# A Hymba-style block: queries and values projected 512 columns wide in K halves, in a new chunk order, with the F, Q and G weights split once and kept in DRAM

## What is computed

```python
h = rmsnorm(x, norm1_w)
proj = h @ w_in                                 # 1024 x 2816
qa, ka, va, qb, fb, ib, gb = split(proj)        # 512, 128, 128, then four of 512
ya = swa_sink_attention(qa, ka, va, ...)        # 8 query heads, 2 key/value heads of 64, window of two 64-token chunks
yb = hgrn2(qb, fb, ib, gb, ...)                 # 4 heads of 128: gated linear recurrence, chunkwise
x = x + concat(ya, yb) @ w_out
gate, up = split(rmsnorm(x, norm2_w) @ w_gate_up)
x = x + (silu(gate) * up) @ w_down              # inner width 2816
```

## Time and profile before

| | us |
|---|---|
| median of 3 runs (lowest, highest) | 2134.61 (2134.19, 2135.76) |
| the profiled execution | 2135.83 |
| its span, first to last instruction | 2134.0 |
| PE busy in the span | 2099.1 |
| DVE busy | 1377.9 |
| ACT busy | 886.0 |
| block 1, from qT 0 at 235.72 to that of block 2 at 402.21 | 166.5 |

### The profile page before, as it was taken

How to read it: one execution, slowest core, us unless ns; L and a number is a source line. 1 busy time by engine, 2 the same in 40 slices (tenths; PEclk the granted TensorE clock), 3 DMA queues, 4 the chain that set the end, 5 groups by cost and what they waited for, 6 DMA issues and landing times.

```text
span 2134.0 us, 28560 instructions
## 1 busy us (share of the span) xinstructions
PE 2099.1 (98%) x11128; PEld 1771.7 (83%) x11128; DVE 1377.9 (65%) x2034; ACT 886.0 (42%) x1490; POOL 105.5 (5%) x108
## 2 busy tenths in 40 slices
PE   7999999999999998999999999999999999999999
PEld 7889879879978787888888888888888888888887
DVE  6666667666577885777777677777677754444332
ACT  5684685585585333432332334333333332222221
POOL 3100200201100000000000000000000000000000
PEclk9999999999999999999999999999999999999999
DMA  7323422523326675444445344645445575654532
GB/s 280 130 75 124 165 80 85 199 80 104 134 86 216 204 263 203 163 133 145 152 158 173 96 146 168 217 143 178 151 144 178 170 253 185 205 179 167 181 134 90
DMA packets 176662, 338.10 MB, mean 158 GB/s; under 512 B 10448, under 2 KB 105936, under 8 KB 161552
## 3 DMA queue, kind: packets, MB, share of 16 engines
q1 hardware_dynamic: 170016, 305.60, 42.4%
q0 software_dynamic: 6512, 30.67, 4.0%
HBM read 233.99 MB, written 102.24 MB: 158 GB/s over the span
## 4 chain that ended last, share of the span: by engine, by line
PE 60%; DVE 0%; DVEq 0%; ACT 0%; issue 0%
PE b_bank_A L351 4%; PE b_bank_A L350 4%; PE b_bank_A L352 4%; PE b_bank_C L351 4%; PE b_bank_B L351 4%; PE b_bank_C L352 4%; PE b_bank_B L350 4%; PE b_bank_C L350 4%; PE b_bank_B L352 4%; PE b_hx_bank L1932 3%; PE b_hx_bank L1930 3%; PE b_hx_bank L1931 3%; PE b_bank_D L350 2%; PE b_bank_D L351 2%; PE b_bank_D L352 2%; PE b_hx_bank L1875 1%
## 5 line engine op out<-in xcount | busy, mean ns | idle before, releaser
L1816 ACT ACTIVATE b_s_hi<-b_s_stage 128x1408 fp32r<-128x1408 f32 x56 | 77.4, 1383 | 300.2 <-PE b_hx_bank L1932 143.7
L350 PE MATMUL a_pj<-a_w_hi,a_hT_hi 128*128 128x256 f32 x640 | 185.7, 290 | 1.5 <-DVE a_hT_lo L1202 1.5
L351 PE MATMUL a_pj<-a_w_lo,a_hT_hi 128*128 128x256 f32 x640 | 181.0, 283 | 0.0
L352 PE MATMUL a_pj<-a_w_hi,a_hT_lo 128*128 128x256 f32 x640 | 180.9, 283 | 0.0
L350 PE MATMUL a_pj<-a_hT_hi,a_w_hi 128*128 128x512 f32 x384 | 154.6, 403 | 6.4 <-ACT a_gT L871 6.0
L352 PE MATMUL a_pj<-a_hT_hi,a_w_lo 128*128 128x512 f32 x384 | 150.1, 391 | 0.0
L351 PE MATMUL a_pj<-a_hT_lo,a_w_hi 128*128 128x512 f32 x384 | 150.0, 391 | 0.0
L350 PE MATMUL b_bank_A<-b_h_hi_B,b_w_hi 128*128 128x512 f32 x352 | 137.9, 392 | 0.0
L351 PE MATMUL b_bank_A<-b_h_lo_B,b_w_hi 128*128 128x512 f32 x352 | 137.5, 391 | 0.0
L350 PE MATMUL b_bank_B<-b_h_hi_T,b_w_hi 128*128 128x512 f32 x352 | 137.3, 390 | 0.0
L352 PE MATMUL b_bank_A<-b_h_hi_B,b_w_lo 128*128 128x512 f32 x352 | 137.3, 390 | 0.0
(11 more groups left out here) (309 smaller groups left out, 5151.6 us busy)
## 6 DMA issues: line engine op xcount, KB each, us to landing
b_gu_stage<-w_gu SPq DMA_DIRECT2D x44, 1024.0 KB, 5.2
a_w_stage<-w_whole SPq DMA_DIRECT2D x40, 1024.0 KB, 5.0
b_s_stage<-a_sums SPq DMA_DIRECT2D x56, 704.0 KB, 4.1
a_sums<-b_a SPq DMA_DIRECT2D x88, 256.0 KB, 5.4
a_sums<-b_gate SPq DMA_DIRECT2D x66, 256.0 KB, 3.9
b_hx<-hc POOLq DMA_DIRECT2D x12, 1024.0 KB, 5.5
b_w_blocks<-w_dn SPq DMA_DIRECT2D x11, 1024.0 KB, 4.9
o_x<-x_pad SPq DMA_DIRECT2D x16, 512.0 KB, 5.3
```

The source lines that it names most:

```text
L350: pe.matmul(out, stationary[0](k), moving[0](k), start=(k == 0 and not adds), stop=False, skip_group_check=adds)
L351: pe.matmul(out, stationary[0](k), moving[1](k), start=False, stop=False, skip_group_check=adds)
L352: last = pe.matmul(out, stationary[1](k), moving[0](k), start=False, stop=(k == ends), skip_group_check=adds)
L1816: act.activation(f.s_hi[n % 2][:], f.s_stage[n % 2][:], ACT.Copy).then_inc(f.s_hi_ready, 1)
```

## The change

**Chunks.** QA0 and QA1 become QAl and QAh: all 512 query columns, first for the lower half of K (4 k), then the upper; I01 and I23 become Il and Ih in the same way. A group has 12 matmuls of 512 columns with the same 128 tokens standing still, and the four groups of a pair stay open in four PSUM banks until the second half is added: `a_pj0`, `a_pj1`, `a_sc0`, `a_sc1` for the queries, `a_pv`, `a_hb`, `a_pj0`, `a_pj1` for the values. pv 0 and att 0, which use `a_pv` and `a_hb`, therefore wait for the eviction of Ih's groups 0 and 1. ACT evicts 512 columns at once, four times instead of eight. The query columns are permuted on the host.

**Kept weights.** In block 0 the chunks F0, F1, F23, Q01, Q23, G01 and G23 are loaded and split as before, and SP then stores w_hi and w_lo to DRAM. In blocks 1 to 3 SP loads both parts from there straight into w_hi and w_lo (kept_load), once PE has finished chunk n - 2; the step stands where the split would. KV, QAl, QAh, Il and Ih are loaded and split in every block.

**Order.** All splits and kept loads now stand at their automatic place; none is placed by hand. o 2 moves to the next block's first group, and the steps are spread over the new chunks as shown. `junk`, the discard tile of the squares, gets a place of its own.

```diff
-CHUNKS = [("KV", 512, 256), ("QA0", 0, 256), ("QA1", 256, 256), ("F0", 1280, 128), ("F1", 1408, 128),
-          ("Q01", 768, 256), ("I01", 1792, 256), ("G01", 2304, 256), ("F23", 1536, 256), ("Q23", 1024, 256),
-          ("I23", 2048, 256), ("G23", 2560, 256)]
+CHUNKS = [("KV", 512, 256), ("QAl", 0, 512), ("QAh", 0, 512), ("F0", 1280, 128), ("F1", 1408, 128), ("F23", 1536, 256),
+          ("Q01", 768, 256), ("Il", 1792, 512), ("Ih", 1792, 512), ("Q23", 1024, 256), ("G01", 2304, 256), ("G23", 2560, 256)]
...
-    after("I01", 0, ("ha", 0), ("split_hi", CHUNK_AT["G01"]))
-    after("I01", 1, ("sm2", 0), ("sm2", 1), ("sc", 1), ("split_lo", CHUNK_AT["G01"]))
-    after("I01", 2, ("pt", 0), ("pt", 1), ("sm1", 2), ("sm1", 3), ("hb", 0))
-    after("I01", 3, ("sm2", 2), ("sm2", 3), ("pv", 0), ("sc", 2))
...
-    after("G01", 3, ("ds", 0, 0), ("ds", 0, 1), ("sm2", 6), ("sm2", 7), ("pv", 2), ("hc", 1))
-    after("F23", 1, ("o", 0), ("on1", 0), ("kt", 1), ("pt", 6), ("pt", 7), ("ha", 2), ("sq", 0))
-    after("Q23", 0, ("pv", 3), ("on2", 0), ("hb", 2), ("split_lo", CHUNK_AT["I23"]), ("ds", 1, 0), ("ds", 1, 1), ("att", 1), ("sq", 1))
-    after("Q23", 1, ("yt", 0), ("hc", 2), ("sq", 2))
-    after("I23", 0, ("o", 1), ("on1", 1), ("ha", 3), ("sq", 3))
-    after("I23", 1, ("on2", 1), ("n1a",), ("kt", 2), ("hb", 3), ("split_lo", CHUNK_AT["G23"]))
-    after("I23", 2, ("yt", 1), ("att", 2), ("hc", 3))
-    after("I23", 3, ("n1b", 0), ("n1b", 1), ("n1b", 2), ("n1b", 3))
-    after("G23", 0, ("ds", 2, 0), ("ds", 2, 1), ("split_hi", NW), ("split_lo", NW))
-    after("G23", 1, ("xT", 0), ("xT", 1))
...
+    after("F23", 0, ("qT", 0), ("qT", 1), ("kT",))
+    after("F23", 1, ("qT", 2), ("qT", 3))
+    after("Q01", 0, ("sc", 0), ("xload",))
+    after("Q01", 1, ("sm1", 0), ("sm1", 1))
+    after("Il", 0, ("ha", 0))
+    after("Il", 1, ("sm2", 0), ("sm2", 1), ("sc", 1), ("hb", 0))
+    after("Il", 2, ("pt", 0), ("pt", 1), ("sm1", 2), ("sm1", 3))
+    after("Il", 3, ("hc", 0), ("ha", 1))
+    after("Ih", 0, ("sm2", 2), ("sm2", 3), ("sc", 2), ("hb", 1))
+    after("Ih", 1, ("pv", 0), ("kt", 0))
+    after("Ih", 2, ("pt", 2), ("pt", 3), ("att", 0), ("sm1", 4), ("sm1", 5))
+    after("Ih", 3, ("hc", 1), ("sm2", 4), ("sm2", 5), ("sq", 0))
+    after("Q23", 0, ("pv", 1), ("ds", 0, 0), ("ds", 0, 1), ("sc", 3), ("sq", 1))
+    after("Q23", 1, ("pt", 4), ("pt", 5), ("o", 0), ("on1", 0), ("sm1", 6), ("sm1", 7), ("ha", 2))
+    after("G01", 0, ("sm2", 6), ("sm2", 7), ("pv", 2), ("on2", 0), ("kt", 1), ("hb", 2))
+    after("G01", 1, ("pt", 6), ("pt", 7), ("att", 1), ("sq", 2), ("hc", 2))
+    after("G01", 2, ("yt", 0), ("ds", 1, 0), ("ds", 1, 1), ("pv", 3), ("ha", 3), ("hb", 3))
+    after("G01", 3, ("kt", 2), ("sq", 3), ("n1a",), ("hc", 3))
+    after("G23", 0, ("o", 1), ("on1", 1), ("n1b", 0), ("n1b", 1), ("n1b", 2), ("n1b", 3))
+    after("G23", 1, ("on2", 1), ("xT", 0), ("xT", 1))
+    after("G23", 2, ("att", 2), ("yt", 1), ("ds", 2, 0), ("ds", 2, 1), ("xT", 2), ("xT", 3))
+    after("G23", 3, ("kt", 3), ("xT", 4), ("xT", 5), ("xT", 6), ("xT", 7))
...
+        following = (b, n + 1) if n + 1 < NW else (b + 1, 0)
+        first_steps = [("split_hi", n + 1), ("split_lo", n + 1)] if following in RAW else [("kept_load", n + 1)] if n + 1 < NW else []
...
+        def store_kept(n):
+            for tile, to in kept_parts(n):
+                sp.dma_start(to, tile).then_inc(w_kept[n % 2], 16)
+
+        def load_kept(b, n):
+            sp.wait_ge(pj_full.sem, pj_full.upto(b, GROUPS_TO[n - 1]))
...
+            for tile, of in kept_parts(n):
+                sp.dma_start(tile, of).then_inc(w_kept[n % 2], 16)
...
+                    elif name in K_HALF:
+                        first_k = K_HALF[name] * (KT // 2)
+                        wide_hi, wide_lo = (part[s][:].rearrange("p a c -> p (a c)") for part in (w_hi, w_lo))
+                        last = three_passes(pe, bank[:], still,
+                                            (lambda k: wide_hi[:, (k - first_k) * 512:(k - first_k + 1) * 512],
+                                             lambda k: wide_lo[:, (k - first_k) * 512:(k - first_k + 1) * 512]), range(first_k, first_k + KT // 2))
```

More of the change, by code:

```diff
@@ L58, with raw_count, staged_count, next_staged @@
 WHOLE_CHUNKS = [n for n in range(NW) if n not in HALF_CHUNKS]
+K_HALF = {"QAl": 0, "Il": 0, "QAh": 1, "Ih": 1}
+SPLIT_ONCE = [n for n, c in enumerate(CHUNKS) if c[0] in FIRST_HEAD]
+RAW = [(b, n) for b in range(NB) for n in range(NW) if b == 0 or n not in SPLIT_ONCE]
+STAGED = [[chunk for chunk in RAW if chunk[1] % 2 == s] for s in range(2)]
+def raw_count(b, n):
+    return RAW.index((b, n)) + 1
+def staged_count(b, n):
+    return STAGED[n % 2].index((b, n)) + 1
+def next_staged(b, n):
+    same = STAGED[n % 2]
+    at = same.index((b, n)) + 1
+    return same[at] if at < len(same) else None
+def kept_count(b, n):
+    s = n % 2
+    return sum(32 for bb in range(b + 1) for m in SPLIT_ONCE if m % 2 == s and (bb < b or m <= n))
 def chunk_name(n):
@@ L113, in block_steps @@
-    after("I23", 2, ("yt", 1), ("att", 2), ("hc", 3))
-    after("I23", 3, ("n1b", 0), ("n1b", 1), ("n1b", 2), ("n1b", 3))
-    after("G23", 0, ("ds", 2, 0), ("ds", 2, 1), ("split_hi", NW), ("split_lo", NW))
-    after("G23", 1, ("xT", 0), ("xT", 1))
-    after("G23", 2, ("o", 2), ("on1", 2), ("kt", 3), ("xT", 2), ("xT", 3))
-    after("G23", 3, ("xT", 4), ("xT", 5), ("xT", 6), ("xT", 7))
-    placed = [step for group in at.values() for step in group if step[0].startswith("split")]
+    after("QAh", 0, ("qn1", 0))
@@ L254, in plan @@
                 if b > 0:
-                    steps += [(b - 1, late) for late in LAST_HEAD.get(place, ())]
+                    steps += [(b - 1, late) for late in LAST_HEADS.get(place, ())]
                 steps += [(b, early) for early in extra.get(place, ())]
@@ L496, in build_phase_a @@
     w_loaded = [sem(f"w_loaded{s}") for s in range(2)]
+    w_kept = [sem(f"w_kept{s}") for s in range(2)]
     x_loaded, rope_loaded = sem("x_loaded"), sem("rope_loaded")
@@ L566, in build_phase_a, with group_bank, wait_bank_free, chunk_cols @@
                "yt": (yH_ready, lambda s: s[1] + 1)}
[L568 to L575 removed]
+    def group_bank(n, g):
+        name = chunk_name(n)
+        if name[0] == "I":
+            return (pvb, hb, pj[0], pj[1])[g]
+        return (pj + sc)[g] if name[:2] == "QA" else pj[(GROUPS_TO[n] + g) % 2]
+    bank_free = {"KV": ((-1, g_ready, 3), (-1, g_ready, 4), (0, kv_ready, 1), (0, kv_ready, 2)),
+                 "QAl": ((0, kv_ready, 3), (0, kv_ready, 4)), "F0": ((0, qa_ready, 1),), "F1": ((0, qa_ready, 2),),
+                 "F23": ((0, f_ready, 1), (0, f_ready, 2)), "Q01": ((0, f_ready, 3), (0, f_ready, 4)),
+                 "Il": (None, None, (0, q_ready, 1), (0, q_ready, 2)), "Q23": ((0, i_ready, 3), (0, i_ready, 4)),
+                 "G01": ((0, q_ready, 3), (0, q_ready, 4)), "G23": ((0, g_ready, 1), (0, g_ready, 2))}
+    def wait_bank_free(pe, b, n, g):
+        free = bank_free.get(chunk_name(n), ())
+        if g < len(free) and free[g] is not None and b + free[g][0] >= 0:
+            back, read, count = free[g]
+            pe.wait_ge(read.sem, read.upto(b + back, count))
     out_banks = [pj + sc, tr + [pvb, hb]]
+    def chunk_cols(n):
+        return P if n in HALF_CHUNKS else WC
     def hT_slot(b, k):
@@ L693, in _ @@
             if kind == "split_lo":
-                n = step[1]
-                if b * NW + n + 2 < NB * NW:
-                    sp.wait_ge(w_lo_ready.sem, w_lo_ready.upto(b, n))
-                    load(n + 2)
+                of, n = (b, step[1]) if step[1] < NW else (b + 1, 0)
+                sp.wait_ge(w_lo_ready, raw_count(of, n))
+                following = next_staged(of, n)
+                if following is not None:
+                    load(following[1])
+                if of == 0 and n in SPLIT_ONCE:
+                    store_kept(n)
+            elif kind == "kept_load":
+                load_kept(b, step[1])
             elif kind == "pv":
@@ L856, in _ @@
                 if kind == "split_hi":
-                    split(b, step[1])
-                elif kind == "proj":
+                    split(*((b, step[1]) if step[1] < NW else (b + 1, 0)))
+                elif kind == "proj" and chunk_name(step[1]) not in ("QAl", "Il"):
                     n, g = step[1:]
-                    name, ps = chunk_name(n), pj[(GROUPS_TO[n] + g) % 2]
+                    name, ps = chunk_name(n), group_bank(n, g)
                     act.wait_ge(pj_full.sem, pj_full.upto(b, GROUPS_TO[n] + g + 1))
@@ L1051, in arrived @@
                             pe.wait_ge(hT_ready.sem, hT_ready.upto(b - 1, k + 1))
-                        last = three_passes(pe, pj[at % 2][:, 0:WC], still, moving, range(KT), arrived if at == 0 else None)
+                        last = three_passes(pe, bank[:, 0:WC], still, (lambda k: w_hi[s][:, k, :], lambda k: w_lo[s][:, k, :]),
```

(1 more changed line is left out.)

164 lines of the change are left out of this document (81 added, 83 removed).

## The result

The changed kernel took 2237.23 us, median of four runs (2235.8 to 2238.84), against 2135.07 for the kernel before on the same chip (four runs): 1.0479 times as long, 95% interval 1.0461 to 1.0497. So it is slower by 102 us where 71 were forecast, 2.2 us above the upper end of the range.

What follows compares the result with a forecast made beforehand. The prediction took TensorE's own instruction stream as the bound, with other engines almost always in time. Width, old waits, kept loads, chains, block ends and clock summed to +71.2 us on the old time: 2206 us, range 2148 to 2235.

Steps and rivals of the forecast that it cites:

- Width: Query and value matmuls: one 512-column matmul takes 12.7 ns less than two narrow ones, 768 pairs in four blocks, -9.8 us.
- Chains A and B: Behind Q01 PE loses 2.1 us at pt 0 and 1, from Il to Ih 3.2 at sc 2; together +21.2 us.
- Chain C: Behind o 0, up to yt 0 and the bank for ds 1: PE loses 3.9 us in each block, +15.6 us.
- Chain D: From yt 0 to the transposes of the next x: PE loses 10.3 us in three blocks, +30.9 us.
- Block 0: Block 0 still splits G01 and G23 inside the stretches behind o 0 and up to the next x transposes, +4 us.
- The last block: It has no next x; its operand copies for the output projection come late instead, +2 us.
- The kept weights: F23's two 1 MB loads land after F1's matmuls end: PE waits 2.75 us in each of three blocks, +8.2 us.
- rival 4: Kept loads bound, late behind w_o stores, 8 us per block: 2140 us without chains (0.02), above 2235 with all (0.05).
- The clock: PE's clock halves after a 9 us stall, costing 2.8 us; three such stalls, +8.3 us.
- rival 1: The stalls from the engines' queue orders come as summed, 2180 to 2235 us; chance 0.55.
- rival 2: The same stalls at about half, since steps overlap better: 2165 us, range 2148 to 2180; chance 0.25.
- rival 3: Everything stays in time, as in the old order, decided at the next x transposes: 2124 us, faster; chance 0.11.

Runs made afterwards that it cites:

- split_all: The changed kernel with nothing kept: all chunks are split in every block, in the new chunk order with 512-column halves; 2233.35 us.
- wo_behind: The changed kernel with the stores of the w_o pieces moved behind F0's kept loads in SP's queue in blocks 1 and 2; 2222.91 us.
- all_three: The changed kernel with softmax steps and Ih's split reordered, next block's layer-norm steps moved to Q23 0, and F chunks split in every block; 2174.41 us.

## Why the prediction came out as it did

The sign, the places and the mechanism were right, the time was 31 us too low. The forecast of idle time was -9.2 + 8.2 + 21.2 + 15.6 + 30.9 + 2 + 4 = +72.7 us, measured +81.1; the forecast of PE's busy time was -9.8 + 8.3 = -1.5, measured +21.9. So three quarters of the miss are in the second.

- **Width, -9.8.** The pace was right (0.2265 us a step); half of the change, alone in the kernel before, gave 5.2 us where 4.9 stood. In the changed kernel halving the matmuls cost only 4.2.
- **Old waits, -9.2.** Gone, as taken.
- **Chains A and B, +21.2.** Measured at pt 0 and 1 1.35 + 0.44 = 1.8 us in block 1 (2.1 forecast), at sc 2 3.16 (3.2).
- **Chain C, +15.6.** 3.54 + 0.94 = 4.5 in a block (3.9 forecast). The prediction added the table loads without the drain that the page "ScalarE: Activation LUTs" of the Trainium skill (section "What ACT_TABLE_LOAD costs") names, by which C and D would, as an estimate, be 4.1 us longer in a block. The trace sides with the 1.28 us of the row: in chain C the next instruction starts 1.29 us behind the start of the load, and the one before ends 0.02 us ahead of it.

```profile
360.02 0.61 ACT L967 ACTIVATE a_t_b<-a_t_b 128x512 f32<-128x512 f32 x1
360.65 1.28 ACT L936 ACT_TABLE_LOAD   x1
361.94 0.60 ACT L936 ACTIVATE a_gT<-a_pj 128x512 f32<-128x512 f32 x1
```

- **Chain D, +30.9.** 24.8 us in three waits, with some 1.2 a block behind it for yt 1's bank: 28.4. The match is luck in part. From yt 0 to the transposes lie 25.3 to 25.5 us where the chain was summed to 23.5, and PE's share of them is 16.3 to 17.7 where 14.3 was taken; the two errors nearly cancel. The low clock behind chain C is in both: the 16 matmuls of ds take 2.08 us at 364.74 and 1.16 at 396.29. The last links are the subtraction of the next KV and the scaling of x_in, as written:

```profile
383.36 2.29 DVE L1257 TENSOR_TENSOR a_w_lo<-a_w_stage,a_w_hi 128x2048 fp32r<-128x2048 f32 x1
385.57 0.16 DVE L1412 TENSOR_SCALAR a_o_ss<-a_o_ss 128x4 f32<-128x4 f32 x1
385.64 2.74 DVE L1266 TENSOR_SCALAR a_x_in<-a_x_in,a_x_rs 128x1024 f32<-128x1024 f32 x4
```

- **Block 0, +4.** It has the 4.1 us at pt 7 that the later blocks don't, and split_all, which splits G01 and G23 in every block, has them in every block.
- **The last block, +2.** The size is near, the reason was not: PE's wait for the operand copies is 0.7 us, less than the 1.3 of the kernel before. In their place come four waits of 0.8 to 1.3 us at y_nat, yH, carry and att_m, 4.5 us together.
- **The kept weights, +8.2: a step that failed.** The term took 2.75 us for F23 in each of three blocks and nothing for F0. Measured: 14.0. In blocks 1 and 2 F0 waits 4.24 and 3.80 us and F23 2.48 and 1.95; in block 3, which has no w_o stores, F1 0.69 and F23 0.89. F23 was near its price; the term's 0.3 us for the wake-up is in no row of PE (at F0 PE starts within 0.1 us of the landing). What failed is the reading of SP's queue: the prediction saw there only "a store of yA or yH, which nobody needs soon", but the w_o stores stand there too, ahead of F0. The prediction had this mechanism among its rivals (rival 4) and gave it 0.05 together with the chains, where wo_behind shows it to be true and worth 14 us. It was priced for all or nothing rather than put into the sum. Its size there, 8 us in each block, was too large.
- **The clock, +8.3: the step that failed most.** The prediction priced three stalls of 9 us at 2.8 each and took nothing for all the others, with no reason given; "2.8 for each of the some 20 stalls" it named only as a bound. With the width at its full 9.8, PE's busy time grew by 21.9 + 9.8 = 31.7 us. The kernel has 13 stalls of 3 us or more in the attention and recurrence stage (B and C in four blocks, D in three, F0 in two) and the one at pt 7 of block 0. At each of these 14 the granted clock fell to its lower level and, from 20 us into the span on, nowhere else in the stage. The windows of these stretches, the three at D and the sum of all 14:

```profile
186.67:196.91 10.24, 5.52 (x17) 4.74 (x18) 6.67 (x9) 1.58 (x3) 1.94 (x1) 0.50 0.30 102
...
384.64:391.47 6.83, 2.95 (x11) 2.76 (x12) 5.33 (x9) 1.38 (x2) 1.94 (x1) 0.50 0.43 154
...
575.79:586.03 10.24, 3.44 (x12) 3.09 (x13) 8.67 (x12) 3.66 (x12) 2.57 (x2) 0.50 0.28 102
...
sum 85.34, PE 63.31 PEld 50.07 DVE 59.61 ACT 21.84 POOL 9.45; mean PE 4.52 PEld 3.58 DVE 4.26 ACT 1.56 POOL 0.67
```

PE did 63.3 us of work there. By the prediction's own rule half of it is the price, 31.7 us; by the steps of 0.43 against 0.23 us it is 47%, 30 us (estimates). So the low clock accounts for the growth of the busy time to within some 2 us. D's three stretches hold 11.9 us, 6 lost, less than the 8.3 forecast; the other 11 stalls cost some 26, and they are what the sum left out. The three repairs of A and B, F and D also returned busy time with the idle time (2121.0 to 2104.4 us in all_three).

What came is rival 1's mechanism, but not its range (2180 to 2235); the time lies where rival 4 with all of the chains had put it, above 2235, and that had 0.05. Without the w_o stores ahead of F0 the kernel takes 2222.9, inside the range. Of rival 2 (chains at half) nothing was seen, and rival 3 was refuted at D, where it said that it would be decided. The signs that the prediction named all came, but for the period of the blocks: given as 17 us longer, it is 22 to 38 longer, for the first transposes of the queries start at 70.77, 275.07, 469.14 and 657.70 us, before at 69.24, 235.72, 402.21 and 568.72. Two signs came that it did not name: a wait at F0 longer than F23's, and the low clock behind B and C.

## What to carry to other kernels

- In a kernel whose main engine is nearly always busy, a step moved in a hand-written order moves everything behind it on every in-order queue. Price each chain from queue order with measured durations: four such chains (A to D) gave stalls within 1.5 us of what the trace showed, D in part by luck. And check a repair the same way, since two of the five reorderings here only moved the stall to the next step in the queue.
- Give each new stall of 3 us or more on TensorE a price for the clock beside the idle time, here 2.3 us each on average (1.5 to 3.3), and put a queue that holds megabytes ahead of a load with a deadline into the sum, not into a rival.
- Split a change that does several things: the wide form alone, made for the queries, was worth 5.2 us and cost no wait, while the order that came with it stood for 71 us of waits (all six new lines but the DMA's).
